# A three-layer model kernel: GpSimd's products, rope, FFN ends and the Mamba-2 scan rearranged

## The reference

```
z, xbc, dt = split(u @ w_in)
xbc = silu(causal_dwconv(xbc) + conv_b);  xs, b, c = split(xbc)
dt = softplus(dt + dt_bias);  a = -exp(a_log) * dt
# chunks of 64 tokens, 4 groups of 8 heads, head width 64, state width 128
seg = exp(acum[l] - acum[s]) for s <= l
y_diag = (c b^T * seg) @ (x * dt)          # inside a chunk
y_off  = exp(acum) * (c @ state)           # from the carried state
state  = state * exp(a_last) + b^T @ (exp(a_last - acum) * x * dt)
y = (y_diag + y_off + d_skip * xs) * silu(z);  y = rmsnorm_by_group(y) @ w_out
```

## Time and profile before

| | |
|---|---|
| runs, median of 3 | 3582.72 us |
| profiled execution | 3577.07 us, span 3575.2 us |
| TensorE busy | 3133.8 us, 88% |
| VectorE, ScalarE, GpSimd busy | 36%, 29%, 11% |
| mean granted clock | 0.943 |

### The profile page before, as it was taken

The page is one execution under the profiler, slowest core; times in us unless marked ns, Lnnn a source line. Parts: engine busy times, 40 slices in busy tenths (PEclk is TensorE's granted clock), DMA queues, the critical chain, the costliest instruction groups (busy, mean ns, idle before and its releaser), DMA issues. The chain is left out here.

```text
span 3575.2 us, 45144 instructions
## 1 busy us (share of the span) xinstructions
PE 3133.8 (88%) x18476; PEld 2403.7 (67%) x18476; DVE 1283.3 (36%) x1522; ACT 1031.3 (29%) x1486; POOL 390.6 (11%) x236
## 2 busy tenths in 40 slices
PE   6987666878757999998878999999999889789999
PEld 4974562323226888786776888788879764678887
DVE  3236741111114332335344332433232455533322
ACT  3115410000003221335223221422232447532222
POOL 3972000000000000100101000100010008210000
PEclk8998888998988999999899999999999999899999
DMA  5433158999973333230013332233223210223322
GB/s 218 146 116 143 39 226 336 427 428 428 428 312 102 94 102 103 67 90 20 2 60 83 94 101 99 83 96 102 95 71 94 82 38 2 85 69 94 94 94 89
DMA packets 301955, 487.07 MB, mean 136 GB/s; under 512 B 15617, under 2 KB 259804, under 8 KB 288494
## 3 DMA queue, kind: packets, MB, share of 16 engines
q1 hardware_dynamic: 297034, 467.35, 37.6%
q10 hardware_dynamic: 2468, 9.20, 0.6%
q0 software_dynamic: 2304, 8.39, 0.6%
HBM read 457.62 MB, written 27.28 MB: 136 GB/s over the span
## 5 line engine op out<-in xcount | busy, mean ns | idle before, releaser
L435 PE MATMUL psum_banks<-u_high,f_ffn_w_high 128*128 128x512 f32 x1408 | 548.5, 390 | 0.7 <-DVE f_ffn_w_low L2690 0.7
L437 PE MATMUL psum_banks<-u_high,f_ffn_w_low 128*128 128x512 f32 x1408 | 548.0, 389 | 0.0
L436 PE MATMUL psum_banks<-u_low,f_ffn_w_high 128*128 128x512 f32 x1408 | 548.0, 389 | 0.0
L2673 DVE TENSOR_TENSOR f_ffn_w_low<-weight_pieces,f_ffn_w_high 128x2048 fp32r<-128x2048 f32 x128 | 293.4, 2292 | 403.4 <-ACT f_ffn_w_high L2634 403.4
L2634 ACT ACTIVATE f_ffn_w_high<-weight_pieces 128x2048 fp32r<-128x2048 f32 x128 | 244.0, 1907 | 325.8 <-PE psum_banks L437 322.1
L435 PEld LDWEIGHTS psum_banks<-u_high,f_ffn_w_high 128*128 128x128 f32 x1408 | 264.5, 188 | 59.1 <-issue 4.2
L437 PEld LDWEIGHTS psum_banks<-u_high,f_ffn_w_low 128*128 128x128 f32 x1408 | 264.4, 188 | 55.2
L436 PEld LDWEIGHTS psum_banks<-u_low,f_ffn_w_high 128*128 128x128 f32 x1408 | 264.5, 188 | 54.4
L435 PE MATMUL psum_banks<-f_ffn_w_high,f_hidden_high 128*128 128x512 f32 x704 | 274.2, 390 | 3.6 <-issue 3.6
L1970 PE MATMUL psum_banks<-expert_ring,experts_x_t 128*64 128x512 f32 x1024 | 241.1, 627 | 37.6 <-DMA expert_ring<-in_expert_w_up 36.0
L437 PE MATMUL psum_banks<-f_ffn_w_high,f_hidden_low 128*128 128x512 f32 x704 | 273.9, 389 | 0.0
(11 more groups left out here) (655 smaller groups left out, 5684.7 us busy)
## 6 DMA issues: line engine op xcount, KB each, us to landing
expert_ring<-in_expert_w_gate SPq DMA_DIRECT2D x32, 2048.0 KB, 35.1
expert_ring<-in_expert_w_up SPq DMA_DIRECT2D x32, 2048.0 KB, 36.3
expert_ring<-in_expert_w_down SPq DMA_DIRECT2D x32, 2048.0 KB, 40.4
weight_pieces<-in_ffn_w_gate SPq DMA_DIRECT2D x88, 512.0 KB, 4.0
weight_pieces<-in_ffn_w_up SPq DMA_DIRECT2D x88, 512.0 KB, 5.3
weight_pieces<-in_ffn_w_down SPq DMA_DIRECT2D x88, 512.0 KB, 4.1
weight_pieces<-in_odd_w_in SPq DMA_DIRECT2D x20, 1024.0 KB, 5.3
mix_in_mod_w<-in_w_ada SPq DMA_DIRECT2D x32, 512.0 KB, 3.6
```

What stands on the lines that cost most here:

```text
L435: nc.tensor.matmul(out, lhs.high, rhs.high, start=start, stop=False, skip_group_check=True)
L436: nc.tensor.matmul(out, lhs.high, rhs.low, start=False, stop=False, skip_group_check=True)
L437: return nc.tensor.matmul(out, lhs.low, rhs.high, start=False, stop=stop, skip_group_check=True)
L2673: nc.vector.tensor_tensor(w.low[:, j], raw[:, j], w.high[:, j].bitcast(F32), ALU.subtract).then_inc(w_low, 1)
```

## The change

- GpSimd's scaling of a modulation piece becomes a product of two tensors, the second being the factor repeated.
- GpSimd rotates all four tiles.
- z is copied by ScalarE alone, through silu (`Through`). Each unit is read by ScalarE only.
- The last two blocks of an FFN's down product go in another order: block n-2 for tiles 0 and 1, block n-1 for 0 and 1, both for tile 2, tile 0's transposes, block n-2 for tile 3, tile 1's transposes, block n-1 for tile 3. ScalarE's and VectorE's order in the seam is written anew. Tile 1 has no dummy products ahead of its turn. Seams without a product in front keep their order.
- Scan: two PSUM banks each for the carried rows and for the mixture's products. Both halves' rows are issued together, the second of unit n and the first of unit n+1. All keys' products are made ahead and copied to SBUF (`cb`). The skip term is added to the mixture's diagonal (`own_x`, four products made ahead) so that xs is not rewritten. GpSimd does the gate. ScalarE's silu is gone from here. VectorE forms the output of unit n-1 behind the mixture of unit n.

```
@@ -219,11 +219,12 @@
         for n in range(self.PIECES):
             q, b = divmod(n, self.BLOCKS)
             pool.wait_ge(self.piece_in[n % 2], (n // 2 + 1) * 16)
-            factor, w, to = self.act[:, 0, q:q + 1], self.w[:, n % 2], self.sums[b]
+            w, to = self.w[:, n % 2], self.sums[b]
+            factor = self.act[:, 0, q:q + 1].unsqueeze(2).to_broadcast([P, self.HALVES, BANK])
             if q == 0:
-                nc.gpsimd.tensor_scalar(to, w, factor, None, ALU.mult).then_inc(self.summed, 1)
+                nc.gpsimd.tensor_tensor(to, w, factor, ALU.mult).then_inc(self.summed, 1)
                 continue
-            nc.gpsimd.tensor_scalar(w, w, factor, None, ALU.mult).then_inc(self.scaled, 1)
+            nc.gpsimd.tensor_tensor(w, w, factor, ALU.mult).then_inc(self.scaled, 1)
             pool.wait_ge(self.scaled, n - self.BLOCKS + 1)
             pool.wait_ge(self.summed, n - self.BLOCKS + 1)
             nc.gpsimd.tensor_tensor(to, to, w, ALU.add).then_inc(self.summed, 1)
...
+                self.reads = (0, 2 * U) if self.conv else (U, 0) if self.sum else (0, U) if self.through else (U // 2, U // 2)
                 self.chunks, self.done, self.freed, self.tiles = before.after if before else (0, 0, (0, 0), 0)
                 self.after = (self.chunks + n, self.done + n * U,
...
                                 convolve(part, c, u)
+                        elif part.through:
+                            if odd:
+                                eng.wait_ge(mm, c * U + (part.done + u + 2))
+                                nc.scalar.activation(part.dest(c, part.units[u]), k.ps[:, u, 0:width(part.units[u])],
+                                                     part.through.function).then_inc(free, 1)
...
+            rope(k, pool, nc.gpsimd, table, tiles, *rope_buffers)
 
         @block.sync
         def _(sp):
...
             nc.vector.tensor_tensor(rest[:], k.ps[:, 6:8, :], bias[:], ALU.add).then_inc(rest_ok, 1)
...
+        if t > 1 or self.ready is None:
+            pe.wait_ge(self.product_ok, t + 1)
+            pe.wait_ge(self.squares, t + 1)
+            keep_busy(self.k, 2 * t, 2)
...
+        if self.ready is not None:
+            branch(0)
+            branch(1)
+            sums(0)
+            scaled(0)
+            sums(1)
+            branch(2)
+            high(0)
+            high(1)
+            branch(3)
+            sums(2)
+            scaled(2)
+            sums(3)
+            high(2)
+            high(3)
             return
         branch(0)
         branch(1)
...
+                    last = down_tile(b, b % 2, a, t, False, b == downs - 1 and a == 1)
+                if b == downs - 1:
+                    last.then_inc(tile_mm, 1)
+
+            for b in range(downs - 2):
+                down(b, b % 2, first=b == 0)
+            for t in (0, 1):
+                down_last(downs - 2, t)
+            for t in (0, 1):
+                down_last(downs - 1, t)
+            down_last(downs - 2, 2)
+            down_last(downs - 1, 2)
+            seam.turn(pe, 0)
+            down_last(downs - 2, 3)
+            seam.turn(pe, 1)
+            down_last(downs - 1, 3)
+            for t in (2, 3):
+                seam.turn(pe, t)
+            seam.settle(pe)
 
         def tile_of(part, t):
...
-        def cb_bank(n):
-            return k.ps[:, 7 if n % 2 else 2, 0:CHUNK]
+        def state_bank(n):
+            return k.ps[:, 2 + n % 2, :]
+
+        def diag_bank(n):
+            return k.ps[:, 6 + n % 2, :]
...
             decays(0)
+            for n, (t, g) in enumerate(units):
+                at = n % (U // 2) * CHUNK
+                for half in range(2):
+                    cols = slice(t * P + half * CHUNK, t * P + (half + 1) * CHUNK)
+                    last = nc.tensor.matmul(k.ps[own(half), 6 + n // (U // 2), at:at + CHUNK], bc_t[:, g, cols], bc_t[:, SSD_G + g, cols],
+                                            start=True, stop=True)
+                if n % (U // 2) == U // 2 - 1:
+                    last.then_inc(cb_mm, 1)
+            pe.wait_ge(s_ok, 1)
+            state_rows(0, 0).then_inc(first_mm, 1)
             for n, (t, g) in enumerate(units):
                 pe.wait_ge(s_ok, 2 * n + 1)
                 pe.wait_ge(x_end_ok, n + 1)
                 for half in range(2):
                     nc.tensor.matmul(k.ps[:, 4 + half, :], b_tok[own(half), t, g * SSD_N:(g + 1) * SSD_N],
                                      x_end[own(half), n % 2, :], start=True, stop=True).then_inc(upd_mm, 1)
-                if n:
-                    pe.wait_ge(y_ok, n)
-                state_rows(n, 0).then_inc(first_mm, 1)
                 if n + 1 < U:
                     decays(n + 1)
                 pe.wait_ge(mixed, n + 1)
+                if n < 2:
+                    pe.wait_ge(cb_ok, 2)
+                else:
+                    pe.wait_ge(y_ok, n - 1)
                 for r in range(R):
                     h = g * R + r
                     for half in range(2):
-                        last = nc.tensor.matmul(k.ps[own(half), 6, r * SSD_P:(r + 1) * SSD_P], mix[own(half), n % 2, r, :],
+                        last = nc.tensor.matmul(diag_bank(n)[own(half), r * SSD_P:(r + 1) * SSD_P], mix[own(half), n % 2, r, :],
                                                 xs[own(half), t, h * SSD_P:(h + 1) * SSD_P], start=True, stop=True)
                 last.then_inc(diag_mm, 1)
                 pe.wait_ge(s_ok, 2 * n + 2)
+                if n:
+                    pe.wait_ge(y_ok, n)
                 state_rows(n, 1).then_inc(off_mm, 1)
+                if n + 1 < U:
+                    state_rows(n + 1, 0).then_inc(first_mm, 1)
 
...
-            def finish(n):
-                g = units[n][1]
-                pool.wait_ge(x_end_ok, n + 1)
-                pool.wait_ge(diag_mm, n + 1)
-                nc.gpsimd.tensor_tensor(heads(part(xs, n)), heads(part(xs, n)),
-                                        skip[:, g * R:(g + 1) * R].unsqueeze(2).to_broadcast([P, R, SSD_P]), ALU.mult).then_inc(skip_ok, 1)
-                pool.wait_ge(skip_ok, n + 1)
+            def gate(n):
                 pool.wait_ge(y_ok, n + 1)
-                nc.gpsimd.tensor_tensor(part(y, n), part(y, n), part(xs, n), ALU.add).then_inc(summed, 1)
+                nc.gpsimd.tensor_tensor(part(y, n), part(y, n), part(z, n), ALU.mult).then_inc(gated, 1)
 
             to_end(0)
             for n in range(U):
...
@@ -3752,6 +3833,11 @@
         @block.vector
         def _(v):
             nc.vector.memset(state[:], 0.0).then_inc(s_ok, 1)
+            for g in range(SSD_G):
+                nc.vector.tensor_tensor(own_x[:, g], k.c("half_ident").unsqueeze(1).to_broadcast([P, R, CHUNK]),
+                                        skip[:, g * R:(g + 1) * R].unsqueeze(2).to_broadcast([P, R, CHUNK]), ALU.mult).then_inc(own_ok, 1)
+            v.wait_ge(cb_mm, 1)
+            nc.vector.tensor_copy(cb[:, 0:U // 2, :].rearrange("p n i -> p (n i)"), k.ps[:, 6, :]).then_inc(cb_ok, 1)
 
             def advance(n, half):
                 g = units[n][1]
...
-            for n, (t, g) in enumerate(units):
-                advance(n, 0)
+            def mixture(n):
+                g = units[n][1]
                 v.wait_ge(seg_ok, n + 1)
+                if n == 0:
+                    v.wait_ge(cb_ok, 2)
+                    v.wait_ge(own_ok, SSD_G)
                 if n >= 2:
                     v.wait_ge(diag_mm, n - 1)
-                nc.vector.tensor_tensor(mix[:, n % 2], seg[:, n % 2], cb_bank(n).unsqueeze(1).to_broadcast([P, R, CHUNK]),
-                                        ALU.mult).then_inc(mixed, 1)
-                if n >= 2:
-                    gate(n - 2)
-                advance(n, 1)
+                nc.vector.tensor_tensor(mix[:, n % 2], seg[:, n % 2], cb[:, n, :].unsqueeze(1).to_broadcast([P, R, CHUNK]),
+                                        ALU.mult).then_inc(decayed, 1)
+                v.wait_ge(decayed, n + 1)
+                nc.vector.tensor_tensor(mix[:, n % 2], mix[:, n % 2], own_x[:, g], ALU.add).then_inc(mixed, 1)
+
+            def output(n):
+                v.wait_ge(first_mm, n + 1)
                 v.wait_ge(off_mm, n + 1)
                 v.wait_ge(diag_mm, n + 1)
-                nc.vector.tensor_tensor(heads(part(y, n)), heads(k.ps[:, 3, :]), per_head(exps, n), ALU.mult).then_inc(scaled, 1)
+                nc.vector.tensor_tensor(heads(part(y, n)), heads(state_bank(n)), per_head(exps, n), ALU.mult).then_inc(scaled, 1)
                 v.wait_ge(scaled, n + 1)
-                nc.vector.tensor_tensor(part(y, n), part(y, n), k.ps[:, 6, :], ALU.add).then_inc(y_ok, 1)
-            gate(U - 2)
-            gate(U - 1)
+                nc.vector.tensor_tensor(part(y, n), part(y, n), diag_bank(n), ALU.add).then_inc(y_ok, 1)
+
+            for n in range(U):
+                advance(n, 0)
+                mixture(n)
+                if n:
```

(60 more changed lines are left out.)

79 lines of the change are left out of this document (40 added, 39 removed).

## The result

The kernel after takes 3550.36 us (median of 4 runs, 3547.36 to 3552.74), the one before, run beside it, 3580.65 (4 runs, 3577.54 to 3583.63). The ratio is 0.9917, with a 95% interval of 0.9903 to 0.9932: 30 us faster, where 10 were forecast. The profiled execution took 3547.36 us (span 3545.5).

What follows compares the result with a forecast made beforehand. TensorE is busy 88% of the span, so gains must come where it waits on a shortened chain. -19 + 0 + 0 - 3 + 12 = -10 from 3577.07, plus 5.65 carried over, gives 3572; range 3554 to 3585.

Steps and rivals of the forecast that it cites:

- part E: Scan rewrite: units of 7.5 us instead of 6.87 and a later start, +12 us, between -2 and +15.
- part C: Silu on z in the projection: ScalarE's extra copies and a table load stay hidden under TensorE, 0, between -1 and +1.
- Part A: Modulation in the first mixer's projection: GpSimd's product at 1.95 us shortens its chunks, -19 us.
- The floor of 148: First mixer's projection: the us TensorE itself needs for chunks 2 to 10, which now take 161.2.
- the four waits of 0.6 at changes of part: First mixer's projection: TensorE waits 0.6 us at each of four changes of part, counted into its time for chunks 2 to 10.
- Rival 3: Modulation: GpSimd's product costs what the sum costs, 2.40 us, both inputs read in full; total -5, 3578; chance 0.19.
- Part B: Rope, all four tiles on GpSimd: VectorE's chain ends earlier but GpSimd is late instead, 0, between -3 and +2.
- Part D: Ends of three FFNs, new order: last transposes start 1 us earlier, -3 in all, between -6 and +2.
- the drop of the clock at tile 2: FFN ends: TensorE idles 2.6 us before tile 2's transposes and drops to the lower clock, 4.35 between sets against 2.6.
- two row products 2.0: Scan unit's chain: the two carried-row products take 2.0 us together.
- The floor of 6.05 us a unit: Scan: the least a unit could take, from today's 6.87 us less TensorE's idle 0.5 and 0.3 of keys' products.
- Rival 1: Scan: the mixture doesn't wait for GpSimd's fade; scan -2, total -24, 3559 us; chance 0.19.

Runs made afterwards that it cites:

- experiment 11: Kernel before with only the GpSimd modulation product change, its second input another whole tile of the tokens instead of the repeated factor: 3564.51 us (one run).
- experiment 10: Kernel after, but VectorE rotates the fourth rope tile again ahead of its copies: 3552.25 us (one run).
- Experiment 1: Kernel before plus a Silu on a 128x2 tile on ScalarE ahead of each convolved part of a projection: 3569.03 us, ratio 0.9968.
- experiment 2: Kernel before with only z put through silu on ScalarE in the projection, and the scan's silu removed: 3570.25 us, ratio 0.9972.
- Experiment 3: Kernel after, with TensorE made to finish the second half's carried rows before issuing the next unit's first half's rows: 3571.31 us (one run).
- experiment 4: Kernel after, with GpSimd's second fade of a unit waiting until VectorE's mixture is complete: 3539.66 us, ratio to before 0.9888.

## Why the prediction was wrong

The forecast was 3572, with a range from 3554 to 3585; the kernel took 3550.36. Two steps failed: part E counted two row products one after the other that run side by side, and part C put its effect on the next loop at nothing. Part A was right as the largest gain, and B and D lie in their ranges.

- **Part A** (-19): the product costs 1.90 (1.95 forecast), the wait ahead of chunk 11 and the low clock behind it are gone. Alone it gives 18.6 by the medians. The total is right, its terms less so. The 1152 products of chunks 2 to 10 take 224.86 - 82.65 = 142.2 us instead of 161.3, where 148 was forecast; the low parts come 15.3 us apart, not 16.6 to 17. Chunk 2 starts 0.2 earlier, not 1.5, and chunk 11 gives 2.5, not 3. That is 21.8 in all, against the 17.5 that I had added up. The floor of 148 was too high by 5.8: the four waits of 0.6 at changes of part don't come (2.4), and from 155 us on 24 products took 2.83 us before and take 2.72 after, for a reason that stays open. (The 139.35 us of the window above leave out the last 24 of the 1152.) Rival 3 is refuted, by the row and by experiment 11. The Trainium skill's GPSIMD Engine Reference, section "3.1 Elementwise — side-by-side cycle accounting", has no discount for a repeated input; these runs show one of 2.40 - 1.90 = 0.50 us at 128x1024, and the measurement decides.
- **Part B** (0): right, 0.4 (experiment 10), and the stage ends with GpSimd's rope, 37 us behind its start, as forecast.
- **Part C** (0, between -1 and +1): wrong, and outside its own range. 7.3 us in the convolved parts and 1.9 in the z part with its start. I looked for the cost of C in the stage that it edits and gave "a table load" a place under TensorE. I did not look at which table the next stage's loop finds. The loop's loads stood in the trace of before, 8 in the convolved part; I had not read that stage by ScalarE's instructions, because no line of it was in the diff. Experiment 1 takes the loads out and leaves the z copies as they were, experiment 2 is part C alone, and both give the gain. The failed step is the 0 of this part: what the loads cost in the next loop, 7.3 us, was not in the sum. The Trainium skill, ScalarE activation tables: per-element evaluation and per-set limits, section "Table sets in the compiler and the runtime", says that the compiler's back end places the loads per block. The traces fit that: in the kernel before the first loop repeats its two loads in each of its four passes, and where a silu has run ahead of the loop (experiments 1 and 2, and the second loop in every kernel) there is none.
- **Part D** (-3): -1.2 to -2.3 an FFN, some -5; the range was -6 to +2. In the third FFN the last transposes come 2648.47 - 2625.35 = 23.1 us behind tile 0's square; with tile 0 complete 5.4 earlier that is 2.3 better than the 20.05 of the earlier trace rows, where 1 was forecast. Tile 1 was on time, and the drop of the clock at tile 2 that I priced didn't come there: its transposes (2645.28) and tile 3's are 3.19 apart, not 4.35. In the first and the second FFN of the same kernel it did come, behind the same wait, and these two seams are 0.8 to 0.9 us longer:

```profile
1449.60 1.97 PE L2386 MATMUL psum_banks<-const_table,weight_pieces 128*128 128x128 f32 x8 [2.65 <-ACT weight_pieces L2424]
```

  So whether this wait of 2.6 us costs the clock changes from one seam to the next, and the forecast's price for it belonged in the sum as a chance.
- **Part E** (+12): wrong, -0.3. The mis-sized term is "two row products 2.0": they measured 1.0, since both, in their new order, write different halves of the PSUM partitions and run side by side. Experiment 3 gives the sum of the forecast back, 7.54. In the earlier trace rows each call had been alone between other work. All the rest of that chain came as forecast, the add's wait among it (1.41 of some 1.6), and so did the late start: the first two periods of update products take 9.58 and 7.19 us, against 6.35 and 6.87, and the first begins 1.5 later, +5 in all; thirteen units of 6.44 give 5.6 back. The floor of 6.05 us a unit had the same term in it: with the add's wait gone as well, a unit takes 5.72 (experiment 4). Rival 1 named the nearest time for a wrong reason: the mixture does wait, as experiment 4 shows.
- **Nobody's part**: in the even layer 5 us go. From the first to the last transposes of the windows, code that is the same in all kernels, takes 43.0 us before, 48.1 after. Both kernels come into it with TensorE at its lower level (1.2 GHz; it has waited for ScalarE and VectorE): the granted clock is 0.55 in the 10 us from 1652 in the kernel before, 0.50 in those from 1631 in the kernel after. Before, the clock is the full one again 10 us behind the first transposes (1652.84; granted 0.94 from 1662 to 1672):

```profile
1662.63 0.94 PE L2812 MATMUL psum_banks<-const_table,windows_p 128*128 128x128 f32 x4
1663.41 1.45 PE L2823 MATMUL psum_banks<-even_va,windows_p_t 128*128 128x64 f32 x12
```

In the kernel after the same products, as far behind the first (1631.22), still run at half the rate (granted 0.50 from 1641 to 1654), and the full clock comes 23 us behind the first:

```profile
1641.16 1.11 PE L2883 MATMUL psum_banks<-const_table,windows_p 128*128 128x128 f32 x4
1642.07 2.66 PE L2894 MATMUL psum_banks<-even_va,windows_p_t 128*128 128x64 f32 x12
```

In three of the thirteen kernels this stage takes 43.0 to 43.4 us, in the other ten 47.3 to 48.2. What decides it was not tried. Another 2.4 us go between the opening of the stage behind the gates and the last low parts of the first FFN's weights, 1140.6 against 1138.2, in code that the change doesn't touch; over the thirteen kernels it is 1138.0 to 1142.6.

## What to carry to other kernels

When an edit changes which functions an engine runs, read the stages behind it too: what state does the next loop find on entry, and what does it reload in each pass? A Silu on 128x2 ahead of the convolved loops of two projections bought 11 us here. Two small products that write different halves of the partitions should stand next to each other, and where VectorE and GpSimd hold each other up, the one with slack should be made to wait for the other.

## What the hardware showed beside it

- Float32 products with 128 rows and 64 output partitions, one for each half of the PSUM partitions: two take 1.08 us adjacent and 2.17 with a wait between them. The Trainium skill, TensorE: Matmul & The Clock Gate, section "Why this matters for your kernels", has small products run at the same time when each output lies in its own group of 32 PSUM partitions. Here the groups are of 64, and the trace agrees. No run has two such products next to each other in the same half.
- GpSimd's product at 128x1024: 1.90 with a repeated second input, 1.89 with the same tile twice, 2.40 with another tile, 2.85 as TENSOR_SCALAR.
- Stages whose code is the same differ by up to 5.2 us from kernel to kernel (43.0 to 48.2 in the windows, 300.1 to 305.3 for the opening of the stage behind the gates without part A), so a gain of that size can't be told from chance by the total alone.
